# Where an expert's rows stand among the 128 partitions: rank bits 0 to 3 on partition bits 2, 4, 5 and 6

## What is computed

```python
g_sel = jnp.argmax(g_logits, axis=-1)
top_val, top_loc = lax.top_k(e_in, TOP_K)              # TOP_K = 2
e_id = g_sel[:, None] * EXPERTS_PER_GROUP + top_loc    # 32 experts
...
def expert_block(args):
    xb = x_pad[idx]                                     # rows of this expert
    hb = jax.nn.silu(xb @ w_e_gate[e]) * (xb @ w_e_up[e])
    return (hb @ w_e_down[e]).astype(jnp.float32) * wts[:, None]
```

## Time and profile before

| | us |
|---|---|
| median of 3 runs | 1129.69 (1128.08 to 1132.62) |
| profiled execution, its own time | 1130.85 |
| its span in the profile | 1129.0 |
| PE busy | 1002.6 (89%) |
| DVE busy | 774.9 (69%) |
| ACT busy | 474.0 (42%) |
| POOL busy | 299.7 (27%) |
| all DMA queues | 197.41 MB, mean 175 GB/s |

### The profile page before, as it was taken

How to read it: one execution, slowest core, us unless ns; L and a number is a source line. 1 busy time by engine, 2 the same in 40 slices (tenths; PEclk the granted TensorE clock), 3 DMA queues, 4 the chain that set the end, 5 groups by cost and what they waited for, 6 DMA issues and landing times.

```text
span 1129.0 us, 13999 instructions
## 1 busy us (share of the span) xinstructions
PE 1002.6 (89%) x5029; PEld 801.8 (71%) x5029; DVE 774.9 (69%) x1241; ACT 474.0 (42%) x860; POOL 299.7 (27%) x347
## 2 busy tenths in 40 slices
PE   5998988998989899999979999849999988888892
PEld 4776767776768678788868888737777766666671
DVE  5557677776777577862455777668988877787771
ACT  5144442233455234322233343325666655555540
POOL 2234132312521422100110212023354332323122
PEclk9999998997999989899989999958999999999996
DMA  7222242111223514424120112937999999999872
GB/s 237 84 85 94 66 142 76 57 56 56 94 75 98 163 58 136 129 71 178 56 63 19 57 57 109 376 135 272 360 363 369 378 362 342 362 336 368 329 251 74
DMA packets 63396, 197.41 MB, mean 175 GB/s; under 512 B 16416, under 2 KB 22976, under 8 KB 50912
## 3 DMA queue, kind: packets, MB, share of 16 engines
q1 hardware_dynamic: 43344, 152.73, 37.4%
q0 software_dynamic: 18688, 39.52, 10.0%
q10 hardware_dynamic: 1296, 4.26, 0.9%
HBM read 190.17 MB, written 37.75 MB: 202 GB/s over the span
## 4 chain that ended last, share of the span: by engine, by line
PE 51%; DMA 18%; DVE 13%; issue 9%; ACT 4%; POOL 3%; SPq 0%; ACTq 0%; POOLq 0%; DVEq 0%
PE bank L946 10%; PE bank L947 9%; PE bank L948 9%; DMA partial_rows<-pg,idh 9%; DMA edr<-w_e_down 4%; PE gu_ps L946 2%; PE gu_ps L948 2%; PE gu_ps L947 2%; PE bank L1017 2%; PE bank L1135 2%; PE y_ps L1330 2%; DMA pg<-partial_rows,idh 2%; DVE egl L1740 1%; DVE Wl L1758 1%; ACT dec L1585 1%
## 5 line engine op out<-in xcount | busy, mean ns | idle before, releaser
L946 PE MATMUL bank<-Wh,hTh 128*128 128x512 f32 x384 | 156.6, 408 | 1.2 <-DVE hTl L1782 1.2
L1740 DVE TENSOR_TENSOR egl<-egr,ghi 128x2048 fp32r<-128x2048 f32 x64 | 143.9, 2288 | 15.0 <-ACT ghi L1400 15.0
L947 PE MATMUL bank<-Wl,hTh 128*128 128x512 f32 x384 | 152.1, 396 | 0.0
L948 PE MATMUL bank<-Wh,hTl 128*128 128x512 f32 x384 | 151.6, 395 | 0.0
L1400 ACT ACTIVATE ghi<-egr 128x2048 fp32r<-128x2048 f32 x64 | 119.6, 1931 | 0.0
L946 PE MATMUL gu_ps<-ghi,xgH 128*128 128x512 f32 x256 | 104.0, 406 | 1.4 <-DVE xgL L2118 1.4
L948 PE MATMUL gu_ps<-ghi,xgL 128*128 128x512 f32 x256 | 101.2, 395 | 0.0
L947 PE MATMUL gu_ps<-egl,xgH 128*128 128x512 f32 x256 | 100.9, 394 | 0.0
L946 PEld LDWEIGHTS bank<-Wh,hTh 128*128 128x128 f32 x384 | 74.0, 193 | 17.8 <-issue 1.6
L1400 ACT ACTIVATE dhi<-edr 128x1024 fp32r<-128x1024 f32 x32 | 33.9, 1060 | 122.9 <-DMA edr<-w_e_down 93.2
L948 PEld LDWEIGHTS bank<-Wh,hTl 128*128 128x128 f32 x384 | 73.6, 192 | 16.2
(11 more groups left out here) (326 smaller groups left out, 2231.7 us busy)
## 6 DMA issues: line engine op xcount, KB each, us to landing
egr<-w_e_gate SPq DMA_DIRECT2D x32, 1024.0 KB
egr<-w_e_up SPq DMA_DIRECT2D x32, 1024.0 KB
edr<-w_e_down SPq DMA_DIRECT2D x32, 1024.0 KB
raw<-w_in SPq DMA_DIRECT2D x50, 256.0 KB, 3.0
xn<-w_in SPq DMA_DIRECT2D x22, 256.0 KB, 3.0
x_sb<-x_prompt SPq DMA_DIRECT2D x8, 512.0 KB, 6.5
partial_rows<-x_sb ACTq DMA_DIRECT2D x8, 512.0 KB, 2.6
ffn_rows<-xn_ffn POOLq DMA_DIRECT2D x8, 512.0 KB, 3.0
```

Source lines behind the costliest of these rows:

```text
L946: pe.matmul(dst, ah, bh, start=first, stop=False)
L947: pe.matmul(dst, ah, bl, start=False, stop=False)
L948: return pe.matmul(dst, al, bh, start=False, stop=last)
L1740: tt(egl[n % 4][:, a, :, :], egr[n % 4][:, a, :, :], ghi[n % 2][:, a, :, :].bitcast(F32), ALU.subtract)\
```

## The change

One instruction: the iota on POOL that writes `iota_s`. Its tile is the same, and so is every instruction behind it; only the numbers in the tile differ.

```diff
-                        pool.iota(iota_s[:, :].rearrange("p (a b) -> p a b", a=16), [[1, 16], [16, 8]], base=0,
-                                  channel_multiplier=0, allow_small_or_imprecise_dtypes=True).then_inc(r_pool, 1)
+                        pool.iota(iota_s[:, :].rearrange("p (a b c d) -> p a b c d", a=8, b=2, c=2),
+                                  [[2, 8], [16, 2], [1, 2], [32, 4]], base=0, channel_multiplier=0, allow_small_or_imprecise_dtypes=True).then_inc(r_pool, 1)
```

## The result

| | before | after |
|---|---|---|
| median, us | 1130.38 (4 runs, 1128.08 to 1132.62) | 1094.29 (4 runs, 1093.70 to 1095.82) |
| profiled execution, us | 1130.85 | 1093.70 |
| its span, us | 1129.0 | 1091.9 |

The ratio is 0.9683, with a 95% interval of 0.9660 to 0.9706: 36 us faster, where 28 were forecast.

A forecast was written before the change was run, and what follows sets the result against it. Eight overloaded DMA engines of 16 were taken to bound the late experts at 11.14 us each, TensorE (9.72) afterwards. Stage and end together gave 27.5 us, all else zero: 1130.85 - 27.5 = 1103.4 profiled, 1102 median, range 1096 to 1115.

The forecast's parts named there:

- The mapping: Row transfers: partition bits 2, 3, 4 and 6 pick the engine; busiest engine falls from 237 rows to 155.
- Prices and the period: Expert stage: fast price 0.163 us a row, so the DMA period falls from 11.14 to 9.9 us.
- lead of 15.6 us: Expert stage: DMAs enter 15.6 us ahead; at 9.9 us 30 experts use 5.4, so TensorE never waits.
- The stage: Experts 11 to 30: 19 late periods shrink to TensorE's 9.72 us, 27.0 us gained.
- The end: Chain of store, copies, POOL's scatters and span end: 25.2 to 30.2 us gained in all, 27.5 taken.
- branches of 25.2 and 30.2: Total gain with old lags at the end (25.2 us), or with the store landing in 9.7 us (30.2).
- The 3 us for copies beside weights: End: copies share the engines with the last weights, some 1 MB or 3 us lost.
- the text's floor: End of the span: cannot be below 1082.0 + 1.3 + 0.3 + 1.3 + 12.8 = 1097.7 us.
- The start: First gather (67 rows) may land half a microsecond sooner, left out; iota 0.37 us, perhaps a few tenths different.
- even load at 10.3 or more: Rival: evenly loaded DMA engines stay the bound; end at 1104 to 1119 us, middle 1112; chance 0.19.
- eight neighbours: Rival: an engine takes eight neighbouring partitions, so the new table is slower, 1137 us; chance 0.05.
- no effect: Rival: lowest four partition bits pick the engine, or store time is latency; 1130 us; chance 0.04.

The follow-up runs named there:

- cut_new: Changed kernel without the product of high rows by low weights in gate and up (8 of 24 matmuls an expert): 1088.38 us.
- r6_on_bit3: Changed kernel with another table, rank bit 6 moved to partition bit 3: 1131.17 us.
- plain: Changed kernel with another table, rank r on partition r, so rank bit 6 on partition bit 6: 1131.18 us.
- old_later_gather: Kernel before (old table), with POOL gathering the sums of expert n at step n instead of n+1: 1130.41 us beside 1130.32.
- after_again: The changed kernel measured again, unaltered, five rounds beside the level table: 1094.48 us, ratio to before 0.9695.
- level: Changed kernel with rank bits 0 to 3 on partition bits 2, 3, 4 and 6 (143 rows on the busiest engine): 1095.26 us, ratio to before 0.9707.
- r6_on_bit5: Changed kernel with another table, rank bit 6 on partition bit 5, rank bits 0 to 3 on bits 2, 3, 4 and 6: 1093.49 us.
- only_bit2: Old table with only rank bits 4 and 6 exchanged, so that partition bit 2 holds rank bit 4: 1095.59 us.
- late_copies: Changed kernel, but SP waits for expert 29's addition before it issues the copies of partial_rows to the outputs: 1106.04 us.
- start_later: Changed kernel, but TensorE's first turn of expert 0's rows also waits for the second gather: 1096.76 us.
- cut kernels: Three kernels without gate and up's product of high rows by low weights: old table 1122.47 us, new table 1088.38, level table 1083.75.
- cut_level: Level table (143 rows on the busiest engine), without the product of high rows by low weights in gate and up: 1083.75 us.

## Why the prediction was right and where it was wrong

The map of partitions to engines, the period and the bound were right. Two terms of the sum were mis-sized, the end and the start, and they put the time 1.7 us outside the range.

- *The mapping.* Right, and 155 rows: bit 3 counts and bit 5 does not.
- *Prices and the period.* Right: 9.9 us, shown by cut_new. TensorE never waited, as was taken. The time of the changed kernel is no test of the 9.9: with a lead of 15.6 us over 30 experts, any DMA period up to 9.72 + 15.6 / 30 = 10.2 us would have given the same.
- *The stage.* 27.9 us against 27.0. The sum took 19 late periods to shrink to 9.72 each; the last of them, expert 29 to 30, has no rows of a next expert to turn and needs 8.82.
- *The end: the step that failed.* "I take 27.5", between branches of 25.2 and 30.2, leaves half a microsecond for the end beyond the stage's 27.0. Measured: 4.2. The mis-sized term is the lag from the last store to the copies, kept at 14.7 us or cut to 9.7 at best. It was 7.1, since a store beside evenly loaded engines lands sooner (3.4 us at least, 11.1 in the median). The 3 us for copies beside weights did not show either: it took 16.7 us from copies to POOL, against 17.2. So the copies were no longer what the end waited for, and the span ended 15.7 us behind the last addition. That is what the text's floor was made of (1.3 + 0.3 + 1.3 + 12.8), but it was taken as a bound and not as the forecast.
- *The start: left out at half a microsecond, and worth 2.9.* Every profile of the full computation with a table that loads eight engines has 32.1 to 32.6 us from table to first addition (before, r6_on_bit3, plain, old_later_gather). Those with a level table have 28.8 to 29.2 (after, after_again, level, r6_on_bit5, only_bit2, late_copies); start_later, which delays the start by design, has 31.4. Of the 2.9 us, 0.9 is the gather of 67 rows. The rest is TensorE's clock, told below, and its cause stays open. The iota itself took 0.63 us and not 0.37, the few tenths that were allowed for it, and nobody waited for it.
- *The rivals.* All fell: even load at 10.3 or more, eight neighbours, no effect.

With 27.9 + 4.2 + 2.9 the sum is 35.0, where 27.5 was taken: 0.9 of the miss is the stage, 3.7 the end and 2.9 the start. The remaining 1 to 2 us between medians and profiles is what such runs vary by. "It cannot be below" 1097.7 failed for the same reasons: the last addition came at 1076.18 and not at 1082.0, and the span ended at 1091.9. Of these 5.8 us, 2.9 are the start, 0.9 the last step and 2.1 the variation ahead of the table.

## What to carry to other kernels

When the DMA share is high but not full and transfers are late, ask whether all engines carry the same: a window in which one partly filled transfer runs alone shows how many take part. Place the rows of a partly filled tile so that its first rows differ in the partition bits that pick the engine. And when a stage's pace changes, work the end out again from its own chain, since a transfer that lands sooner can take a whole chain off the path: here the end gained 4.2 us beside the 27.9 of the pace.

## What the runs showed that was not expected

In the full kernels with tables that load eight engines, TensorE's granted clock stands at 0.50 in two stretches at the start of the experts, and with the others in one. These windows are from the kernel before:

```profile
766.00:768.00 2.00, 2.00 (x10) 1.67 (x9) 1.90 (x6) 0.00 (x0) 0.00 (x0) 0.93 0.41 103
...
770.00:772.00 2.00, 1.14 (x21) 0.95 (x18) 2.00 (x2) 2.00 (x5) 1.61 (x1) 1.00 0.89 233
772.00:774.00 2.00, 0.34 (x2) 0.37 (x3) 1.93 (x6) 0.07 (x1) 1.19 (x1) 0.78 1.03 434
774.00:776.00 2.00, 2.00 (x10) 1.90 (x9) 1.99 (x4) 0.95 (x2) 0.12 (x1) 0.50 0.99 418
776.00:778.00 2.00, 2.00 (x10) 1.64 (x9) 0.86 (x2) 2.00 (x3) 0.87 (x1) 0.87 1.04 428
```

and these from the changed kernel, at the same work:

```profile
760.00:762.00 2.00, 2.00 (x7) 1.58 (x6) 1.93 (x4) 1.98 (x2) 2.00 (x1) 0.60 0.68 197
762.00:764.00 2.00, 2.00 (x11) 1.63 (x10) 1.73 (x9) 0.32 (x1) 1.41 (x2) 1.00 0.38 96
...
766.00:768.00 2.00, 1.41 (x23) 1.20 (x21) 2.00 (x2) 2.00 (x4) 1.35 (x1) 1.00 0.69 193
768.00:770.00 2.00, 0.07 (x1) 0.10 (x2) 1.97 (x5) 0.34 (x3) 1.45 (x1) 1.00 1.00 418
770.00:772.00 2.00, 2.00 (x13) 1.82 (x14) 1.97 (x5) 1.29 (x3) 0.67 (x1) 1.00 1.01 430
```

The clock rises from 0.50 (1.2 GHz) to 1.00 (2.4 GHz) some 5 us after the first matmul of gate and up before, and 3 us after. It falls again to 0.50 near 774 us only before; TensorE had paused for 2.5 us just ahead of it, and it pauses as long in the changed kernel without a fall. From that first matmul to expert 0's addition it is 23.65 us before, 21.6 after, and 22.0 in start_later, which rises late but does not fall; so the second stretch costs about 1.7 us, an estimate. It is there in all four full kernels with loaded engines and in none of the seven others. But all three cut kernels show it too, two of them with tables that load all engines; this is cut_level:

```profile
772.00:774.00 2.00, 2.00 (x12) 1.71 (x11) 2.00 (x4) 1.53 (x3) 0.90 (x1) 0.77 0.98 414
774.00:776.00 2.00, 2.00 (x6) 1.59 (x5) 1.31 (x3) 2.00 (x2) 0.17 (x1) 0.50 1.01 426
776.00:778.00 2.00, 2.00 (x9) 1.58 (x9) 2.00 (x2) 1.16 (x1) 0.00 (x0) 0.88 0.84 324
```

So loaded engines are not needed for it. What starts it stays open, and with it by what way the table gives the 2 us at the start.

The other surprise is plain at 11.11 us with 252 rows on its busiest engine, no slower than the old table with 237. In the one case where the price per row was carried beyond the old table's load, it gave too much; why is not shown.
